# Two mixer stages of a two-block transformer kernel: the gates are copied out of PSUM first, and their sigmoids are computed later, in one row

## The reference, cut to what matters

```
(aq, ak, av, hy, gq, gk, gv, go, glr, gates) = split_cols(hn @ w_in[i], IN_SPLITS)
y_a = attention_mixer(...) @ w_br_attn[i]
y_b = hyena_mixer(...) @ w_br_hyena[i]
y_c = gla_mixer(...) @ w_br_gla[i]
gate = jax.nn.sigmoid(gates.reshape(B, L, N_BRANCH, D_MODEL))
mixed = gate[:, :, 0] * y_a + gate[:, :, 1] * y_b + gate[:, :, 2] * y_c
h = h + mixed @ w_out[i]
h = h + memory_cross_attention(...)
h = h + square(relu(rmsnorm(h) @ mlp_w1[i])) @ mlp_w2[i]
```

## Time and profile before

| | us |
|---|---|
| median of 3 runs | 3614.75 |
| lowest, highest | 3612.49, 3620.67 |
| the profiled execution's own time | 3614.83 |
| its span, first to last instruction | 3613.0 |
| TensorE busy | 3411.1 |
| ScalarE busy | 1773.1 |
| VectorE busy | 2105.9 |

### The profile page before, as it was taken

The page is one execution under the profiler, slowest core; times in us unless marked ns, Lnnn a source line. Parts: engine busy times, 40 slices in busy tenths (PEclk is TensorE's granted clock), DMA queues, the critical chain, the costliest instruction groups (busy, mean ns, idle before and its releaser), DMA issues.

```text
span 3613.0 us, 56474 instructions
## 1 busy us (share of the span) xinstructions
PE 3411.1 (94%) x23510; PEld 3112.3 (86%) x23510; DVE 2105.9 (58%) x3178; ACT 1773.1 (49%) x2696; POOL 636.4 (18%) x260
## 2 busy tenths in 40 slices
PE   5898999999999899999999997999999989999899
PEld 5766999997888779999988884979989968899899
DVE  6525785655777556946645556465645455755443
ACT  3514556664444445566655443445445424544462
POOL 0000586660000003976620000000000000000000
PEclk8989999999999999999999998999999989999999
DMA  6233454447887333554456553322534614244254
GB/s 242 71 117 132 146 180 151 140 143 243 278 274 255 128 113 132 181 160 140 141 180 193 194 194 113 140 97 106 186 121 161 179 46 147 99 150 168 103 186 130
DMA packets 265234, 565.59 MB, mean 157 GB/s; under 512 B 15055, under 2 KB 91155, under 8 KB 264211
## 3 DMA queue, kind: packets, MB, share of 16 engines
q1 hardware_dynamic: 264980, 561.99, 47.1%
HBM read 560.89 MB, written 1.05 MB: 156 GB/s over the span
## 4 chain that ended last, share of the span: by engine, by line
PE 84%; DVE 6%; ACT 3%; DMA 2%; POOL 2%; issue 1%; SPq 0%; DVEq 0%; ACTq 0%
PE ps L372 9%; PE ps L374 9%; PE ps L373 9%; PE ps L1746 7%; PE ps L1747 7%; PE ps L1748 7%; PE ps L1825 6%; PE ps L1827 6%; PE ps L1826 6%; PE ps L1792 3%; POOL uvr_split L2125 2%; DVE ring_split L445 1%; PE ps L818 1%; PE ps L502 1%; PE ps L2282 1%
## 5 line engine op out<-in xcount | busy, mean ns | idle before, releaser
L2125 POOL TENSOR_TENSOR uvr_split<-uvr,high_split 128x1024 fp32r<-128x1024 f32 x172 | 431.9, 2514 | 1126.3 <-ACT high_split L1871 1126.3
L1748 PE MATMUL ps<-consts_sb_split,uvr_split 128*128 128x256 f32 x2048 | 579.1, 283 | 0.0
L1871 ACT ACTIVATE high_split<-uvr 128x1024 fp32r<-128x1024 f32 x342 | 360.9, 1056 | 246.6 <-PE ps L1827 210.0
L374 PE MATMUL ps<-uvr_split,ring_split 128*128 128x256 f32 x1680 | 477.1, 284 | 0.0
L1747 PE MATMUL ps<-ht_split,high_split 128*128 128x256 f32 x1488 | 425.3, 286 | 0.0
L445 DVE TENSOR_TENSOR ring_split<-big,high_split 128x2048 fp32r<-128x2048 f32 x111 | 251.8, 2268 | 277.6 <-ACT high_split L437 276.3
L1746 PE MATMUL ps<-consts_sb_split,high_split 128*128 128x256 f32 x1392 | 403.3, 290 | 6.8 <-DVE ht_split L577 3.8
L445 DVE TENSOR_TENSOR ring_split<-big,hot_split 128x2048 fp32r<-128x2048 f32 (+2 forms) x111 | 248.6, 2240 | 267.8 <-ACT hot_split L437 266.3
L1826 PE MATMUL ps<-uvr_split,hot_split 128*128 128x512 f32 x1024 | 400.8, 391 | 0.0
L1748 PEld LDWEIGHTS ps<-consts_sb_split,uvr_split 128*128 128x128 f32 x2048 | 392.0, 191 | 0.0
L488 ACT ACTIVATE big<-ps 128x512 f32<-128x512 f32 (+1 forms) x226 | 132.4, 586 | 425.8 <-PE ps L374 231.5
(11 more groups left out here) (442 smaller groups left out, 8689.3 us busy)
## 6 DMA issues: line engine op xcount, KB each, us to landing
uvr<-peer_uv SPq DMA_DIRECT2D x512, 512.0 KB, 3.9
big<-mlp_w SPq DMA_DIRECT2D x32, 2048.0 KB
big<-w_in SPq DMA_DIRECT2D x26, 2048.0 KB
uvr<-mod_w SPq DMA_DIRECT2D x56, 512.0 KB, 6.1
big<-mod_w SPq DMA_DIRECT2D x10, 2048.0 KB
big<-peer_w_q SPq DMA_DIRECT2D x8, 2048.0 KB
big<-hy_w_in SPq DMA_DIRECT2D x7, 2048.0 KB
big<-x_wk SPq DMA_DIRECT2D x4, 2048.0 KB
```

Of the source, the lines that this page charges most:

```text
L374: m = mm(out, wl, x_high[:, k, :], start=False, stop=en)
L1748: return mm(out, w_low, x_high, start=False, stop=stop, **kw)
L1871: SE.activation(expert_high(e), expert(e), ACT.Copy).then_inc(S["expert_high"], 1)
L2125: GE.tensor_tensor(expert_low(j), expert(j), expert_high(j).bitcast(F32), ALU.subtract)\
```

## The change

The twelve gate evictions of a mixer become copies (same banks, same destinations), and free the bank under another signal, "gate_copied". A new function `open_gate(k)` applies the sigmoid in SBUF, in four instructions of 128x512, each of which sends the "gate_in" that VectorE's multiplications wait for, and each waited for by ScalarE before the next. It is called for all three gates right behind `gate_in(2, 3)`. Three of the calls of `logs_and_exps()` in the stretch go: the one ahead of the decay's exponential and the two ahead of the norms' logarithms. The one behind the Silu and the one behind the last gate stay. TensorE's, VectorE's and SyncE's programs are as before.

```
-                yield from split_steps("gate", x_high, x_low, DC, D, "act", "gate_in")
+                yield from split_steps("gate", x_high, x_low, DC, D, "act", "gate_copied")
...
             def gate_in(k, q):
-                evict_act([z.gates[k][:, 2 * q:2 * q + 2, :]], ACT.Sigmoid, frees="gate_in")
+                evict_act([z.gates[k][:, 2 * q:2 * q + 2, :]], frees="gate_copied")
                 split_high()
+
+            def open_gate(k, n=4):
+                for q in range(n):
+                    g = z.gates[k][:, 2 * q:2 * q + 2, :]
+                    SE.activation(g, g, ACT.Sigmoid).then_inc(S["gate_in"], 1)
+                    SE.wait_ge(S["gate_in"], S.nth(SE, "gate_in"))
...
                 if o == 1:
-                    evict_act([z.gates[0][:, 4:6, :]], ACT.Sigmoid, frees="gate_in")
+                    evict_act([z.gates[0][:, 4:6, :]], frees="gate_copied")
...
                 if o == 0:
-                    logs_and_exps()
                     SE.wait_ge(S["logit_abs"], S.nth(SE, "logit_abs"))
...
             gate_in(1, 1)
-            logs_and_exps()
             roots_act(z.mem_rs, 1, D)
...
             gate_in(1, 2)
-            logs_and_exps()
             roots_act(z.rs, 4, 128.0)
...
             for q in range(2, 4):
                 gate_in(2, q)
+            for k in range(3):
+                open_gate(k)
             logs_and_exps()
             for _ in range(6):
                 split_high()
```

## The result

| | before | after |
|---|---|---|
| median of 5 runs, us | 3614.75 | 3633.3 |
| lowest, highest | 3612.49, 3620.67 | 3632.81, 3636.09 |
| span of the profiled execution | 3613.0 | 3634.1 |

The ratio is 1.005, with an interval from 1.0036 to 1.0065. Beside other kernels the changed one was timed twice more: 3637.55 against 3616.01 (1.0061, 1.0047 to 1.0074) and 3634.78 against 3615.34 (1.0058, 1.0044 to 1.0072). The profiled execution of the changed kernel took 3636.09 us, the longest of its five, so that the spans differ by more (21.1 us) than the medians (18.55).

What follows compares the result with a forecast made beforehand. TensorE, busy 94% of the span and 84% of the chain, was taken to bound the kernel. Loads and evictions 0, row 13.6, clock 4.2, longer wait 0.5: 18.3 us on 3614.8 gives 3633.1 us, range 3626 to 3640.

Steps and rivals of the forecast that it cites:

- The row: Twelve sigmoids and two loads behind the last gate make the next high part late; TensorE waits 6.8 us a layer, 13.6 in all.
- The clock: Behind TensorE's 6.8 us wait its granted clock falls, costing 1.4 or 2.7 us; 2.1 us a layer taken, 4.2 in all.
- Evictions as copies: Gate evictions on ScalarE: copies cost at most 0.03 us more each than sigmoids, covered by idle time; 0 us.
- Loads that go: Gate stretches: 16 fewer loads take 20.6 us off ScalarE, but the transfer for piece (2,2) holds TensorE's start; gain 0 us.
- The longer wait at (2,2): TensorE's two short waits at (2,1) and (2,2) join into 3.33 and 2.03 us; extra clock loss 0.5 us for both layers.
- loads on the path: Rival: ScalarE sets the pace in the gate stretches, so 16 loads give back 20.6 us: 3594 us; chance 0.03.
- row covered: Rival: TensorE sees none of the row's delay, or under 3.6 us a layer: 3611 to 3622 us; chance 0.05.
- clock costs more: Rival: TensorE at 1.2 GHz for the whole late piece and again after it: 3639 to 3642 us; chance 0.06.
- The 9.5 us of waiting: TensorE's wait behind the row, per layer, if a table switch cost the skill page's 2.66 us; sum 23.7 us, not adopted.

Runs made afterwards that it cites:

- spreading the row: Changed kernel with 2, 4, 4 and 2 sigmoids ahead of the first four high parts, then the load of the logarithm and exponential set: 3614.36 us, ratio 0.9997.
- rows of eight and ten: Changed kernel with eight or ten of the twelve sigmoids ahead of the first high part, the others in twos ahead of the next: 3625.47 and 3628.71 us.
- filling the idle time: Changed kernel with 54 extra, unread TensorE matmuls ahead of the second branch's first piece, where TensorE waits: 3630.53 us, 7.0 below the changed kernel of its set.
- the early slot: Kernel before the change, with the memory tensor's slot ahead of the second gate instead of the third in the order of weights: 3608.5 us, ratio 0.9984.
- both kernels with the loads put back: Changed kernel with the nine removed loads of a layer put back: 3631.02 us; the same plus a forced sigmoid-set load ahead of the row: 3632.54 us.
- the kernel with spread sigmoids and the early slot: Changed kernel with sigmoids spread 2, 4, 4, 2 over the high parts and the memory tensor's slot ahead of the second gate: 3611.01 us, ratio 0.9991.

## Why the prediction was right

The median was 3633.3 for 3633.1 forecast, and the mechanism was the one forecast: a late high part behind the row, TensorE waiting for it, and a slow clock behind the wait. By steps, on the profiled executions:

- *The row.* 7.3 us of lateness, 0.5 of slack, 6.8 of waiting. The twelve sigmoids took 7.9 us, as forecast, and the wait was 6.82 in all three traces of the changed kernel, or 6.9 from restart to restart. Shown by spreading the row (gone) and by rows of eight and ten (2.89, 4.21). Two layers: 13.8 us for 13.6.
- *The clock.* 2.1 in a layer, between 1.4 and 2.7. Measured 2.7 and 1.6, 4.3 for 4.2; shown by filling the idle time.
- *Evictions as copies.* 0 was forecast. They were not changed alone; spreading shows that all of the exchanged work together is 0 within the interval.
- *Loads that go.* 0 for the time, and 0 was measured. The reason given was only half of it. The chain of the changed kernel at piece (2,2):

```profile
2499.67 8.93 DMA big<-w_in
...
2512.43 2.21 DVE ring_split L445
```

  The transfer is there, released by TensorE at the same point as before. The chain of before gave it 6.65 us and left 2.40 us ahead of ScalarE's start as "issue", which the prediction passed over; here the chain gives it 8.93 us up to that start, and the early slot shows that it set the start in the kernel before too. But behind it VectorE's order would have taken the 0.81 us back just the same.
- *The longer wait at (2,2).* 0.5 us for both layers was too little. The first layer had 3.54 us for 3.33 and lost no more clock than before. The second had 2.39 for 2.03, and the halved clock behind it (0.72), where the kernel before and both kernels with the loads put back have 1.00: from (2,2) to the first late piece it is 3254.96 - 3223.56 = 31.4 us against 3236.2 - 3213.3 = 22.9 before, 8.5 more, of which the row is 6.9. So this term is 1.6 us, three times what was forecast.

13.8 + 4.3 + 1.6 = 19.7 us. The spans differ by 21.1. Of the other 1.4 us some 0.4 is the second layer's longer wait at (2,2) itself; the rest lies outside these stretches, where halved clock stretches behind other waits came out longer or shorter: between the two mixers TensorE's lag behind the kernel before went from 9.7 us down to 6.8 and up again to 10.1. That the median met the forecast so closely is partly luck: the two other sets put the changed kernel 21.5 and 19.4 us above the kernel before.

Of the rivals, "loads on the path" is refuted by spreading and by putting the loads back, "row covered" by the wait of 6.82 us, "clock costs more" by the stretches. The rule of the Trainium skill, ScalarE: Activation LUTs, section "Table sets: the hidden batching unit", to batch activations by set was followed by the edit and did not pay here: the trace has 16 loads fewer, at 1.29 us each, and a later end. The 9.5 us of waiting that the prediction worked out from that page's price of a switch did not come either: it was 6.82. The page does not say on which side of the load its drain stands; the rows show none on either side, as the load at 2499.82 starts 0.02 us behind the activation before it (2498.74 + 1.06) and ends 0.01 us ahead of the next.

## What to carry to other kernels

Before grouping an engine's work to save table loads, look at what is queued behind the group and how much idle time stands there: here 3.15 us of room and 0.5 of slack against 10.5 us of load, row and load. What a load costs is decided by what waits for it. Of the twelve loads that went with the gate evictions eight come right behind ScalarE's wait for TensorE, like this one in ScalarE's timeline before the change:

```profile
2457.98 1.28 ACT L488 ACT_TABLE_LOAD   x1 [4.60 <-PE ps L374]
```

So they do delay the eviction and the high part behind it. They were free all the same, as TensorE's timeline shows no wait that hangs on them; the only one that does, 0.81 us, belongs to a load that stands behind no idle time, at 2499.82. The load that now stands ahead of the row is on the path with all of its length. If a group must be made, cut it to the size of the idle times between the pieces that the bounding engine waits for. And if a removed wait comes back at the next piece, look for the second cause behind the first, as each one hides the next.

## What the runs showed of the hardware

A set switch costs its own 1.28 us and nothing visible more: the next activation starts 1.29 to 1.30 us after the load's start.

The same wait of 6.82 us cost 2.7 to 2.8 us of clock in the first layer and 1.6 to 1.7 in the second, in all three traces of the changed kernel. Waits of 2.39 and 2.52 us were already followed by a halved clock, at 0.72 and 0.73 over the next 6 us, those of 2.89 us behind the row of eight at 0.75 and 0.72, while 2.84 us at the inverse transform was not in the kernel before: no fall is recorded behind it in either layer. But in both kernels with the loads put back the same wait of 2.83 or 2.84 us was, in the second layer, and the same 32 matmuls took 8.83 us in place of 7.14. So the length of a wait alone does not say whether the clock falls.

The 11 executions of the kernel with spread sigmoids and the early slot took between 3601.12 and 3614.4 us, the 12 with the early slot alone between 3603.94 and 3616.49, wider bands than the changed kernel's 5 executions in any set. The granted clock goes with it: its mean was 0.973 in the fastest of the 11, the profiled one, and 0.969 or 0.970 in the five slowest. What moves it from one execution to the next was not settled.
